# A front rearranged: the first norm's sums on DVE, the modulation tiles after the input, and the first head's projections beside H

## The reference

```python
# first block, one layer: modulation from the conditions, a norm, one wide projection
mod = silu(c) @ w_mod + b_mod                       # shift, scale, gate, ... each 1024 wide
h = modulate(rms_norm(x, norm1_g), sh1, sc1)        # rms_norm(x) * g * (1 + scale) + shift
hc = modulate(rms_norm(ctx, norm1_g), csh1, csc1)
# token mixer: eight heads of a gated delta rule over chunks, in two directions
p = h @ w_in                                        # k | v | ba (32 columns) | q | z | u | ...
q, k, v, beta, g = delta_prep(p, conv_qkv, a_log, dt_bias, True)
gc = jnp.cumsum(g, axis=-1)                         # then exp(gc_i - gc_j) masks k k^T and q k^T
m = jnp.where(strict, jnp.einsum('nbhid,nbhjd->nbhij', kb, k) * gamma, 0.0)
t_inv = lax.linalg.triangular_solve(eye + m, ...)   # the inverse, here in six levels
...
```

## Time and profile before

| | |
|---|---|
| runs | 3159.66, 3165.8, 3174.3 us; median 3165.8 |
| profiled execution | 3164.87 us, its span 3163.2 us |
| TensorE busy | 3010.3 us, 95% of the span |
| VectorE, ScalarE, GpSimd busy | 1037.8, 727.3, 222.4 us |
| granted TensorE clock, mean | 0.978 |

### The profile page before, as it was taken

One profiled execution on the slowest core, in us unless ns is written; L12 is line 12 of the kernel. 1 busy time (PEld: TensorE's weight loads), 2 busy tenths in 40 slices (PEclk: granted clock), 3 DMA queues, 4 the chain that ended last, 5 costly groups with the idle time before them and its releaser, 6 DMA issues.

```text
span 3163.2 us, 41650 instructions
## 1 busy us (share of the span) xinstructions
PE 3010.3 (95%) x16950; PEld 1730.5 (55%) x16950; DVE 1037.8 (33%) x2035; ACT 727.3 (23%) x1436; POOL 222.4 (7%) x280
## 2 busy tenths in 40 slices
PE   7999999999999999999988998999999999999998
PEld 2777777666444444444435556665555545575443
DVE  1555555454212224445112115531101332352011
ACT  3333343332200002221003215530000031362000
POOL 0222221111000000000001001000000010100000
PEclk8999999999989999999999999999999999999999
DMA  5000000002423333444231111001111121101222
GB/s 189 24 28 22 28 28 28 28 28 95 132 68 133 131 101 120 154 158 151 88 95 47 47 40 38 1 21 47 53 47 47 53 67 47 57 1 47 73 73 73
DMA packets 59846, 214.05 MB, mean 68 GB/s; under 512 B 6401, under 2 KB 8577, under 8 KB 59442
## 3 DMA queue, kind: packets, MB, share of 16 engines
q1 hardware_dynamic: 42512, 153.11, 15.2%
q0 software_dynamic: 13344, 50.59, 4.8%
q10 hardware_dynamic: 3842, 8.19, 0.7%
HBM read 208.20 MB, written 2.10 MB: 66 GB/s over the span
## 4 chain that ended last, share of the span: by engine, by line
PE 90%; DVE 4%; ACT 2%; issue 2%; DMA 1%; POOL 0%; ACTq 0%; DVEq 0%
PE psum L338 87%; PE psum L704 2%; DMA arena<-in_ctxT 1%; DVE arena L1313 1%; DVE arena L1578 0%; DVE arena L1296 0%; DVE arena L1293 0%; POOL arena L1725 0%; DVE arena L1301 0%; ACT arena L941 0%; DMA arena<-in_ctx2T 0%; DVE arena L1564 0%; PE psum L534 0%; ACT arena L1149 0%; ACT arena L1104 0%
## 5 line engine op out<-in xcount | busy, mean ns | idle before, releaser
L338 PE MATMUL psum<-arena 64*64 64x64 f32 (+7 forms) x16150 | 2914.0, 363 | 143.1 <-ACT arena L874 19.5
L338 PEld LDWEIGHTS psum<-arena 128*128 128x128 f32 (+4 forms) x16150 | 1643.2, 162 | 1393.4 <-issue 1180.9
L1423 DVE SCALAR_TENSOR_TENSOR arena<-arena 128x1024 f32<-128x1024 f32 x128 | 149.2, 1219 | 3.7 <-DMA arena<-in_mods 3.7
L1671 DVE SCALAR_TENSOR_TENSOR arena<-arena,psum 128x512 f32<-128x512 f32 x32 | 21.2, 685 | 381.5 <-PE psum L338 381.5
L1104 ACT ACTIVATE arena<-psum,arena 128x512 f32<-128x512 f32 (+2 forms) x160 | 115.5, 728 | 58.9 <-DVE arena L1570 22.4
L1163 ACT ACTIVATE arena<-psum 128x512 f32<-128x512 f32 x32 | 19.1, 598 | 382.2 <-PE psum L338 382.2
L704 PE MATMUL psum<-arena 128*128 128x128 f32 x704 | 98.0, 284 | 1.1 <-ACT arena L1104 0.9
L704 PEld LDWEIGHTS psum<-arena 128*128 128x128 f32 x704 | 77.8, 143 | 29.2 <-issue 24.7
L1739 POOL DMA_DIRECT2D arena<-in_mods x76 | 40.2, 529 | 690.6 <-DVE arena L1423 690.6
L1725 POOL TENSOR_TENSOR arena<-arena 128x256 f32<-128x256 f32 x96 | 75.9, 808 | 162.3 <-DVE arena L1332 91.7
L1092 ACT ACTIVATE arena<-psum 128x512 f32<-128x512 f32 (+1 forms) x128 | 56.4, 489 | 86.0 <-PE psum L704 85.8
(11 more groups left out here) (196 smaller groups left out, 1338.3 us busy)
## 6 DMA issues: line engine op xcount, KB each, us to landing
arena<-in_stream SPq DMA_DIRECT2D x288, 512.0 KB, 3.5
arena<-in_mods POOLq DMA_DIRECT2D x80, 512.0 KB, 3.6
arena<-in_bias POOLq DMA_DIRECT2D x16, 384.0 KB, 3.9
arena<-in_xT ACTq DMA_DIRECT2D x1, 2048.0 KB, 20.3
out<-arena SPq DMA_DIRECT2D x1, 2048.0 KB, 7.2
arena<-in_conds ACTq DMA_DIRECT2D x1, 1536.0 KB
arena<-arena POOLq DMA_DIRECT2D x4, 384.0 KB, 4.3
arena<-in_ctxT ACTq DMA_DIRECT2D x1, 1024.0 KB, 26.2
```

What stands on the lines that cost most here:

```text
L338: return pe.matmul(out, lhsT, rhs, start=start, stop=stop, skip_group_check=True)
L1423: m = stt(mjunk[:, b % 2, :] if x < len(conds) - 1 else slot, slot, 0.5, cb[:, c, :], ALU.mult, ALU.mult, accum_out=dst(x))
```

## The change

There are two parts. In the first, the first norm's squares are summed on DVE: ScalarE squares X[k] into a buffer of its own (`first_sq`, in the place of S and what follows it), DVE adds it to a running sum (`sqsum`), and TensorE does one product with ones for all eight, behind modulation tile 13. TensorE also waits for x and the context before it takes tile 4. In the second, TensorE's order from H on is another one: behind the gate product of each k stands the same step of head 0's k projection; all of q stands behind the `sum4` products; two steps of v stand between the cumulated gates and their transposes, the other six behind the transposes. Head 0 then skips q and v in the head loop. To free banks the cumulated gates move to bank 3 and the context's transposed gates to bank 2.

```diff
-STREAMED = {1: 0, 2: 1, 4: 2}
-SQUARED = {0: 0, 3: 1}
+STREAMED = {0: 0, 1: 1, 2: 2, 4: 3}
...
             for t in range(16):
                 k, hf = divmod(t, 2)
+                if t == 4:
+                    pe.wait_ge(s("x_in"), 32)
                 w = weights(pe, T_PRE + t)
...
-                if 6 <= t < 6 + KT:
-                    norm_step(0, t - 6, (1, 2))
+                if t == 13:
+                    norm_sums(0, (1, 2), True)
...
                 m = mm(psum[r:r + 32, 6, 0:CTX], wba[:, k, :], H[:, k, SEQ:TOK], k < 4, k >= 4)
-            m.then_inc(s("front"), 1)
-            steps(T_HEAD, range(0, 1), 0, 1, 0)
+                if k == KT - 1:
+                    m.then_inc(s("front"), 1)
+                steps(T_HEAD, range(k, k + 1), 0, 1, 0)
             pe.wait_ge(s("front_rows"), 3)
             for c in range(CH):
                 m = mm(psum[:, 3, 32 * c:32 * c + 32], ba_rows[:, c * P:(c + 1) * P], sum4)
             m.then_inc(s("front"), 1)
-            steps(T_HEAD, range(1, KT), 0, 1, 0)
+            steps(T_HEAD + 1, range(KT), 4, None, 0)
             pe.wait_ge(s("g"), 1)
             for d in range(2):
-                mm(psum[:, 4, 48 * d:48 * d + 48], tri[:, d, :], gt[:, 0, :, 8 * d:8 * d + 8])
-            mm(psum[:, 4, 96:192], ones, flat(gt[:, 0])).then_inc(s("gcum"), 1)
+                mm(psum[:, 3, 192 + 48 * d:240 + 48 * d], tri[:, d, :], gt[:, 0, :, 8 * d:8 * d + 8])
+            mm(psum[:, 3, 288:384], ones, flat(gt[:, 0])).then_inc(s("gcum"), 1)
+            steps(T_HEAD + 2, range(0, 2), 6, 7, 0)
             pe.wait_ge(s("gc"), 2)
             for c in range(CH):
                 for r in (0, 32):
-                    m = mm(psum[r:r + 16, 5 + c // 4, (c % 4) * P:(c % 4 + 1) * P], gt[:, 1, c, :], ident)
+                    m = mm(psum[r:r + 16, 2 if c >= XC else 5, (c % 4) * P:(c % 4 + 1) * P], gt[:, 1, c, :], ident)
             m.then_inc(s("gcum"), 1)
+            steps(T_HEAD + 2, range(2, KT), 6, 7, 0)
...
                 if i:
                     pe.wait_ge(s("oln"), i)
-                steps(T_HEAD + 1, range(KT), 4, None, i)
+                    steps(T_HEAD + 1, range(KT), 4, None, i)
...
             act.wait_ge(s("x_in"), 32)
-            norm_squares(0)
+            for k in range(KT):
+                if k >= 2:
+                    act.wait_ge(s("sqsum"), k)
+                f(first_sq[:, k % 2, :], X[:, k, :], ACT.Square).then_inc(s("nsq"), 1)
             norm_root(0, (1, 2), True)
...
+            squares_begin(0)
+            for k in range(KT):
+                dve.wait_ge(s("nsq"), k + 1)
+                dve.wait_ge(s("sqsum"), k + 1)
+                tt(sqb[:, 1, :], sqb[:, 1, :], first_sq[:, k % 2, :], ALU.add).then_inc(s("sqsum"), 1)
             dve.wait_ge(s("used"), 16)
```

More of the change, by code:

```diff
@@ L165, in build @@
         qg = hp.take(2, SEQ)
+        S_AT = hp.at
         S = hp.take(2, 6, P)
@@ L172, in build @@
         condp = flat2(eR)[:, 0:KT * 32].rearrange("p (k n) -> p k n", k=KT)
+        first_sq = arena[:, S_AT:S_AT + 2 * TOK].rearrange("p (a b) -> p a b", a=2)
         pre_rows = flat2(ktok)[:, 0:SEQ]
@@ L364, in norm_sums @@
                 for k in range(KT):
[L365 to L372, removed]
+                    pe.wait_ge(s("nsq"), KT + k + 1)
+                    mm(psum[:, banks[0], 0:SEQ], ones, sqb[:, k % 2, 0:SEQ], k == 0, k == KT - 1)
+                    m = mm(psum[:, banks[1], 0:CTX], ones, sqb[:, k % 2, SEQ:TOK], k == 0, k == KT - 1)
+                    m.then_inc(s("nsum" if k == KT - 1 else "sq_read"), 1)
             def steps(t, ks, bank, ctx_bank, i):
@@ L482, in _ @@
                 pe.wait_ge(s("ob"), i + FREE)
-                steps(T_HEAD + 2, range(0, 3), 6, 7, i)
+                if i:
+                    steps(T_HEAD + 2, range(0, 3), 6, 7, i)
                 pe.wait_ge(s("squares"), 2 * i + 2)
                 mm(psum[:, 4, :], ones, sqq[:, 0:SEQ]).then_inc(s("ssum"), 1)
-                steps(T_HEAD + 2, range(3, 6), 6, 7, i)
+                if i:
+                    steps(T_HEAD + 2, range(3, 6), 6, 7, i)
                 pe.wait_ge(s("kq"), 2 * i + 1)
@@ L498, in _ @@
                 m.then_inc(s("ktr"), 1)
-                steps(T_HEAD + 2, range(6, KT), 6, 7, i)
+                if i:
+                    steps(T_HEAD + 2, range(6, KT), 6, 7, i)
                 pe.wait_ge(s("ln"), 2 * i + 2)
@@ L867, in _, with norm_squares @@
             f = act.activation
-            def norm_squares(n):
+            def norm_squares():
                 for k in range(KT):
                     if k >= 2:
-                        act.wait_ge(s("sq_read"), (KT - 1) * SQUARED[n] + k - 1)
+                        act.wait_ge(s("sq_read"), k - 1)
                     f(sqb[:, k % 2, :], X[:, k, :], ACT.Square).then_inc(s("nsq"), 1)
@@ L925, in _ @@
                 f(gcT[r:r + 16, 0:SEQ], psum[r:r + 16, 5, :], ACT.Copy)
-                f(gcT[r:r + 16, SEQ:TOK], psum[r:r + 16, 6, 0:CTX], ACT.Copy).then_inc(s("gcTs"), 1)
+                f(gcT[r:r + 16, SEQ:TOK], psum[r:r + 16, 2, 0:CTX], ACT.Copy).then_inc(s("gcTs"), 1)
             for i in range(HEADS):
@@ L1129, in _ @@
                 if l == 0:
-                    norm_squares(3)
+                    norm_squares()
                 norm_root(3 + l, (0, 1), True)
@@ L1198, in squares_add @@
                 tt(sqb[:, 0:1, 0:w], xk, xk, ALU.mult).then_inc(s("sq"), 1)
-                dve.wait_ge(s("sq"), k + KT * at + 1)
+                dve.wait_ge(s("sq"), k + KT * (at - 1) + 1)
                 tt(sqb[:, 1:2, 0:w], sqb[:, 1:2, 0:w], sqb[:, 0:1, 0:w], ALU.add).then_inc(s("sqsum"), 1)
@@ L1264, in _ @@
             dve.wait_ge(s("gcum"), 1)
-            dve.tensor_copy(gt[:, 1, :, 0:8], psum[:, 4, 0:48].rearrange("p (c n) -> p c n", c=CH))
-            dve.tensor_copy(gt[:, 1, :, 8:16], psum[:, 4, 48:96].rearrange("p (c n) -> p c n", c=CH))\
+            dve.tensor_copy(gt[:, 1, :, 0:8], psum[:, 3, 192:240].rearrange("p (c n) -> p c n", c=CH))
+            dve.tensor_copy(gt[:, 1, :, 8:16], psum[:, 3, 240:288].rearrange("p (c n) -> p c n", c=CH))\
                 .then_inc(s("gs"), 1)
@@ L1270, in _ @@
             tt(gA[:, 1], gt[:, 4], gt[:, 1], ALU.subtract).then_inc(s("gc"), 1)
-            tt(gt[:, 11], psum[:, 4, 96:192].rearrange("p (c n) -> p c n", c=CH), gt[:, 1], ALU.subtract)\
+            tt(gt[:, 11], psum[:, 3, 288:384].rearrange("p (c n) -> p c n", c=CH), gt[:, 1], ALU.subtract)\
                 .then_inc(s("gc"), 1)
```

## The result

The changed kernel takes 3173.18 us in the median of 12 runs (3170.78 to 3179.09), the kernel before 3170.55 in 12 runs beside it. The ratio is 1.0024, with a 95% interval of 1.0014 to 1.0033: 7.6 us more, between 4.4 and 10.5. The two medians taken by themselves are only 2.6 us apart and the means 5.5, so the sign is sure and the size is not. I had forecast 6.4 more on the profiled execution, and a change within 0.5%. The profiled execution took 3173.65 us, its span is 3172.0, 8.8 over the span before.

A forecast was written before the change was run, and what follows sets the result against it. TensorE, busy 95% of the span, was taken as the bound: only product work and its idle or low-clock stretches count. Terms -9.5 + 18.0 - 1.4 - 0.7 = +6.4 us gave 3171 us, range 3160 to 3181.

The forecast's parts named there:

- Up to L: From the start to the last modulation tile done: earlier input and norm sums off TensorE save 9.5 us.
- rival of starved tiles: Modulation tiles: streamed tiles land only every 2.0 us, adding 3.8 us to the forecast, 3175 us; chance 0.12.
- From H0 to R: First product on H to head 0's decay rows ready: k, q and v moved ahead add 18.0 us.
- rival of overlapping narrow products: H stretch: narrow gate products half overlap with wide k products, 4.6 us less, 3167 us; chance 0.18.
- From R to M: Head 0's decay rows ready to DVE's first mask multiply: filling spent, kk cold, net 1.4 us less.
- rival in which only the gates are hidden: Head 0: TensorE's work merely moves, later chain finds cover, front gain and gate waits saved, 3152 us; chance 0.04.
- Behind M: After DVE's first mask multiply of head 0: v's last two steps no longer precede level 0, 0.7 us less.
- The clock stays down: Inverse of head 0: TensorE stays at 1.2 GHz after its idle stretches, 13 us more, 3184 us; chance 0.04.

The follow-up runs named there:

- four-step kernel: Against q in the gaps: four steps of v, not three, before the sum of q's squares in heads 1 to 7 too; 0.9961 of the kernel before.
- q in the gaps: Against the first part alone: head 0 has four q steps in TensorE's waits, four v steps before q's square sum; 0.9974, again 0.9962 of the kernel before.

## Why the prediction was right, point by point

The sum was -9.5 + 18.0 - 1.4 - 0.7 = +6.4; the profile has -7.1 + 19.0 - 1.2 - 0.8 = +9.8 up to level 0 of head 0 (unrounded), and the time +7.6.

- **Up to L**, -9.5: right in sign, a third too large. The input came as said (24.6 for 24.45), the sums on DVE were done long before tile 13. The mis-sized term is the stream's: I took a lone transfer's 3.3 us to landing and then 1.31 us a tile, at 400 GB/s. From 32 to 38 us the DMA share was 0.92 and the stream moved only 304 GB/s, 1.7 us a tile. With several transfers out a landing takes 5.0 in the median and 6.4 at most, and tiles 8 to 15 were taken up at 30.46 to 42.77 us, 1.76 apart in the mean with the norm's sums among them. My cold start of tile 4 was wrong too (the clock was 1.00), but it gave time only to tiles that then waited for the next. The truth lies between my forecast and the rival of starved tiles.
- **From H0 to R**, +18.0: 19.0. The stretch with k took about 24.7 us (its last pair starts at 70.40), more than the 23.8 that I had as forecast and as upper bound at once. A pair costs 2.90 and not 2.70, 1.6 us in eight pairs; the cold first pair gave 0.7 of it back (4.42 us, 1.5 over a warm one, where I had 2.2). The columns of a pair are 2.56, so two switches cost 0.34, not the 0.14 that I took from the old alternation, where the 32-column side was two products in different column groups. The drain that *TensorEngine Tiling (Array Packing)* of the Trainium skill names (Key Properties) agrees with this; that the 0.34 is this drain and nothing else was not shown. The rival of overlapping narrow products is out. That the gate chain is hidden, and that the decay rows wait 5 us behind v, came as written: DVE done at 88.74, rows at 96.49.
- **From R to M**, -1.4: -1.2, with kk cold, which keeping TensorE busy confirmed. The rival in which only the gates are hidden is out: nothing fills that stretch.
- **Behind M**, -0.7: -0.8.
- **The clock stays down** did not happen: cold until some 1.6 us behind M, warm again from 117.

What my sum did not hold is the rest of the kernel. I had written that I am wrong if anything behind M in heads 1 to 7 moves by more than the shift, and it did: between head 0 and head 7, M was delayed by another 2.5 us (below). Behind head 7 the span of the changed kernel is 4.3 us shorter (2455.1 against 2459.4 us). So the chain up to M was right, and that the whole came out near my number is in part luck: +2.4 and +1.0 of error in the first two terms, +2.5 in the heads and -4.3 behind them. Over all profiles of this study that last stretch is 2451.8 to 2464.1 us long, a spread larger than the effect of the change, with code that is the same in all but the four-step kernel. It was not settled what makes it vary; the granted clock has cold stretches there of different lengths.

## What to carry to other kernels

Work can be moved beside a wait for nothing only if nobody behind it in the queue is due sooner: filling belongs into the idle time itself, and no longer than it, or it makes the next chain late and is missing as cover afterwards. Price a transfer by its time to landing with as many transfers out as there will be, not by that of a lone one. A narrow product between full-width ones had to be paid in full here, in float32, and 0.34 us a pair on top.

## What the runs showed of the hardware

**GpSimd and DVE side by side.** At level 3 of a head GpSimd's mask multiplies run beside two DVE operations on SBUF. Head 0 of the kernel before, then of the changed one:

```profile
120.13 2.13 POOL L1725 TENSOR_TENSOR arena<-arena 128x256 f32<-128x256 f32 x2 [2.31 <-PE psum L338]
...
120.22 1.45 DVE L1301 SCALAR_TENSOR_TENSOR arena<-arena 128x768 f32<-128x768 f32 x1
...
122.22 1.18 POOL L1731 TENSOR_TENSOR arena<-arena 128x256 f32<-128x256 f32 x1
```

```profile
130.24 0.95 DVE L1314 SCALAR_TENSOR_TENSOR arena<-arena 128x768 f32<-128x768 f32 x1
...
130.27 2.66 POOL L1738 TENSOR_TENSOR arena<-arena 128x256 f32<-128x256 f32 x2 [2.44 <-PE psum L339]
...
132.89 0.73 POOL L1744 TENSOR_TENSOR arena<-arena 128x256 f32<-128x256 f32 x1
...
134.33 0.68 PE L339 MATMUL psum<-arena 64*64 64x64 f32 x15 [0.82 <-issue]
```

Before, GpSimd starts 0.09 us ahead of DVE and DVE's operation takes 1.45 us instead of 0.95. In the changed kernel DVE starts 0.03 ahead, keeps its 0.95, and GpSimd's pair takes 2.66 instead of 2.13. *GPSIMD Engine Reference* of the Trainium skill says (Specifications, the row on SBUF interfaces) that GpSimd shares its SBUF interface with DVE instructions that have two SBUF inputs; that fits both lengths, though no run here took the contention away.

**The heads that became longer.** In the kernel before, the M of two heads are 85.64 us apart, seven times the same to 0.01. In the changed one the distances are 86.12, 85.66, 86.36, 85.69, 86.05, 85.70 and 86.34. It goes with the first part: the second part alone has 85.57 in the mean, every kernel with the first part and three steps of v has 85.75 to 86.07. The contention is not shown to be the cause. GpSimd's third multiply is the shorter one in the changed kernel (0.73 for 1.18), so all three end 3.35 us after the first began, against 3.27. TensorE then stands idle for 0.82 us, but the profile puts this down to "issue", no wait that it shows, and TensorE goes on only 0.7 us after the last mask is done. In heads 2, 4 and 6 GpSimd is behind DVE because it waited longer for TensorE (2.64 to 2.67 us for 2.31), so TensorE was late already. And with q in the gaps, GpSimd is ahead in heads 0 and 4, which are still followed by 86.16 and 86.32. Idle times of TensorE of this kind (0.82, 0.35 and 0.37 us) stand 19.3 to 19.7 us behind the M of heads 0, 2 and 6 of the changed kernel, and in no head of the two kernels without the first part. In the kernel kept busy, which differs from the changed one only by products put into TensorE's queue before M of head 0, the two longest distances stand behind heads 1 and 5 instead. What holds TensorE there stays open. What is shown is that the same loop body came out up to 0.7 us longer in every second head after an edit elsewhere, which a forecast that takes it as fixed leaves out.
